# Two decoder layers in one program: layers without a barrier, the root mean square applied at the bank, rotary halves swapped by transfers, weights contiguous in order of use

## The reference, cut to what matters

```python
def hybrid_layer(x, ...):                       # x is (1, 512, 1024), float32; DEPTH = 2 layers
    h = rms_norm(x, ln_g)                       # x * rsqrt(mean(x*x) + eps) * ln_g
    u = einsum('bsd,de->bse', h, w_in)          # 20*256 + 4 + 4*1024 columns
    o_sb = stick_breaking_attention(q_sb, k_sb, v_sb)                       # 4 heads of 64
    o_fx = forgetting_attention(rms_norm(q_fx), rms_norm(k_fx), v_fx, log_f)
    o_dl = dilated_mixture(rope(rms_norm(q_dl)), rope(rms_norm(k_dl)), v_dl)  # 12 heads
    o_mm = memory_cross_attention(rms_norm(q_mm), km, vm)   # km, vm from rms_norm(mem)
    y_b = (o_b * silu(z_b)) @ w_br_b            # for each of the four branches b
    merged = sum_b sigmoid(gate_b) * y_b
    return x + merged @ w_out
```

## Time and profile before

| | |
|---|---|
| median of 3 runs | 1473.55 us (1472.71 to 1476.11) |
| the profiled execution | 1473.23 us, of which the span is 1471.4 us |
| mean granted clock | 0.966 of 2.4 GHz |
| DMA | 115.68 MB, mean 79 GB/s |

### The profile page before, as it was taken

How to read it: one execution, slowest core, us unless ns; L and a number is a source line. 1 busy time by engine, 2 the same in 40 slices (tenths; PEclk the granted TensorE clock), 3 DMA queues, 4 the chain that set the end, 5 groups by cost and what they waited for, 6 DMA issues and landing times.

```text
span 1471.4 us, 18405 instructions
## 1 busy us (share of the span) xinstructions
PE 1366.6 (93%) x6264; PEld 1051.6 (71%) x6264; DVE 506.0 (34%) x762; ACT 688.0 (47%) x1278; POOL 708.7 (48%) x586
## 2 busy tenths in 40 slices
PE   6998999998999999999979899999889999999997
PEld 4766867865667788887757578777656668888876
DVE  5687231233331122222248843213332301222232
ACT  4554522476444544444335534226654445444432
POOL 5556631343332366676355566213432424676662
PEclk8999999998999999999989989999899999999998
DMA  5422321121222144444243224112112222344432
GB/s 177 124 74 65 102 63 37 36 51 43 51 58 56 46 110 104 108 109 115 72 124 101 65 72 108 35 31 51 44 49 52 58 57 64 99 110 108 104 115 96
DMA packets 206974, 115.68 MB, mean 79 GB/s; under 512 B 8212, under 2 KB 200980, under 8 KB 206872
## 3 DMA queue, kind: packets, MB, share of 16 engines
q1 hardware_dynamic: 206872, 114.42, 29.6%
HBM read 108.10 MB, written 6.29 MB: 78 GB/s over the span
## 4 chain that ended last, share of the span: by engine, by line
PE 49%; issue 18%; POOL 14%; DVE 8%; ACT 7%; DMA 2%; SPq 1%; ACTq 0%; POOLq 0%; DVEq 0%
PE dense L715 32%; PE score L715 9%; POOL w_lo L1596 7%; PE acc L715 3%; POOL normed L1629 3%; ACT w_hi L1118 3%; DVE turned L1438 3%; PE out L715 2%; DMA w_raw<-in_w_in 2%; POOL o_norm L1637 1%; POOL inv_den L1637 1%; PE turn L715 1%; DVE negmax L1481 1%; POOL dk_lo L1641 1%; PE turn L840 1%
## 5 line engine op out<-in xcount | busy, mean ns | idle before, releaser
L1596 POOL TENSOR_TENSOR w_lo<-w_raw,w_hi 128x512 fp32r<-128x512 f32 (+1 forms) x398 | 481.9, 1219 | 611.4 <-ACT w_hi L1118 595.7
L715 PE MATMUL dense<-h_hi,w_hi 128*128 128x512 f32 x1168 | 507.7, 435 | 29.9 <-DVE h_lo L1327 15.9
L715 PE MATMUL dense<-h_lo,w_hi 128*128 128x512 f32 x1168 | 466.2, 399 | 0.0
L715 PE MATMUL dense<-h_hi,w_lo 128*128 128x512 f32 x1168 | 466.0, 399 | 0.0
L715 PEld LDWEIGHTS dense<-h_hi,w_hi 128*128 128x128 f32 x1168 | 225.9, 193 | 116.4 <-DVE h_lo L1327 19.0
L715 PEld LDWEIGHTS dense<-h_lo,w_hi 128*128 128x128 f32 x1168 | 226.0, 194 | 50.6 <-issue 11.5
L715 PEld LDWEIGHTS dense<-h_hi,w_lo 128*128 128x128 f32 x1168 | 225.3, 193 | 50.8
L1118 ACT ACTIVATE w_hi<-w_raw 128x512 fp32r<-128x512 f32 (+1 forms) x398 | 225.9, 586 | 53.9 <-PE dense L715 51.0
L1333 DVE TENSOR_SCALAR sig<-sig 128x512 f32<-128x512 f32 x64 | 48.3, 755 | 262.2 <-ACT sig L1173 262.2
L1247 ACT ACTIVATE probs<-score 128x512 f32<-128x512 f32 (+1 forms) x48 | 27.2, 575 | 110.4 <-PE score L715 110.3
L1382 DVE COPY raw<-dense 128x512 f32<-128x512 f32 (+1 forms) x48 | 31.8, 663 | 118.3 <-PE dense L715 118.3
(11 more groups left out here) (280 smaller groups left out, 1939.5 us busy)
## 6 DMA issues: line engine op xcount, KB each, us to landing
w_raw<-in_w_in SPq DMA_DIRECT2D x296, 256.0 KB, 2.9
w_raw<-in_w_out SPq DMA_DIRECT2D x32, 256.0 KB, 2.8
x_scratch<-v_dil SPq DMA_DIRECT2D x16, 256.0 KB, 3.6
w_raw<-in_w_mem_kv SPq DMA_DIRECT2D x16, 256.0 KB, 2.8
v_dil<-x_scratch SPq DMA_DIRECT2D x16, 256.0 KB, 2.7
silu_z<-in_mem SPq DMA_DIRECT2D x4, 512.0 KB, 4.0
w_raw<-in_w_br_dil SPq DMA_DIRECT2D x16, 128.0 KB, 2.3
w_raw<-in_w_br_sb SPq DMA_DIRECT2D x16, 128.0 KB, 2.2
```

The source lines that it names most:

```text
L715: return nc.tensor.matmul(o, lhsT, rhs, start=start, stop=stop, skip_group_check=True)
L1596: pool.tensor_tensor(w_lo[:, n % SPLIT_SLOTS, c], w_raw[:, n % RAW_SLOTS, c], f(w_hi[:, n % SPLIT_SLOTS, c]), ALU.subtract).then_inc(w_lo_ ...
```

## The change

Seven things are changed.

1. **No barrier.** The hardware loop is gone: both layers are written out one after the other, semaphores count on (`Signal.of(key, ago)`), weight items are numbered through both layers, and `end_layer` and the early loads are dropped.
2. **Root mean square at the bank.** `h` becomes x times the gain alone. It is made as soon as x is there: in layer 0 for each half of the tokens while x is still coming in, in layer 1 behind each `o` tile. Each dense tile computed from h is multiplied by 1/rms (`x_rstd_row`) when DVE reads it from its bank. For normed tiles this takes the place of ACT's two reads (ACT now squares `raw`); for gates it is an added instruction (ACT used to read the bank itself). `x_sum` moves into the first tile of the layer. In layer 0 the sum of squares comes from ACT along the token rows.
3. **Rotary halves by transfers.** The four copies become four transfers SBUF to SBUF of 32 x 512 floats, issued on ACT's queue. `post3` of t+1 issues them; sine, cosine and add move to `post4` of t+1, behind the next tile's first half and ahead of `post2` of t+2; rounding and low part move to a new `post5` behind the second half. `turned` has two buffers, `normed` still one.
4. **Weights.** They are laid out in device memory block after block in order of use, so that a partition's 2 KB are contiguous (four runs of 512 B before). Number and bytes of the loads are the same.
5. **Gates.** `cap` and `log_exp` of a gate move from `post1` to `post2`.
6. **Start and constants.** The first weight item is loaded behind the second quarter of x, the large constants behind the first four items; `pick` is one column for each head, broadcast as the stationary operand.
7. **End.** The transposes of x go between the last `o` tiles: 16 behind the fifth, 12 within the last, 4 behind it; stores are by halves.

The core of the diff:

```diff
@@ plan_layer, dense()
             if h == 0:
-                rope = waiting[4]
+                for r in waiting[4]:
+                    add("post4", r)
+                waiting[5] += waiting[4]
                 waiting[4] = []
                 while len(waiting[2]) >= lag and not (...):
                     waiting[3].append(waiting[2].pop(0))
                     add("post2", waiting[3][-1])
-                for r in rope:
-                    add("post4", r)
             if h == len(t.items) - 1:
                 add("post1", t)
                 for r in waiting[3]:
                     add("post3", r)
+                for r in waiting[5]:
+                    add("post5", r)
...
-    for kt in range(KT):
-        add("h", kt)
-    add("h_end")
-    dense([new(kind, DIL, i) for kind in "qk" for i in range(6)], lag=2)
+    dense([new(kind, DIL, i) for kind in "qk" for i in range(6)], [("room",), ("x_sum",)] + [("room",)] * 14, lag=2)
...
-    dense([new("o", None, dt) for dt in range(KT)])
-    for j in range(EARLY):
-        add("early", j)
-    add("x_sum")
+    dense([new("o", None, dt) for dt in range(HALF + 1)])
+    add("out", 0)
+    dense([new("o", None, dt) for dt in range(HALF + 1, KT - 1)])
+    dense([new("o", None, KT - 1)], [("room",), ("out", 1)])
+    add("out", 2)
@@ sync
+                src = w_stream[g, :, c]
+                sp.dma_start(dst, src).then_inc(w_in_sem[g % RAW_SLOTS], 16)
...
-                for n in range(RAW_SLOTS):
-                    load_item(n, (l + 1) % DEPTH, w_next_in)
-                sp.wait_ge(w_next_in, 16 * RAW_SLOTS)
-                sp.wait_ge(layer_done, 4)
-                sp.sem_clear(range(layer_sems[0].num, layer_sems[-1].num + 1))
-                sp.sem_inc(layer_go, 1)
@@ scalar
                     elif kind == "post1" and s[1].kind == "o":
...
+                        act.activation(h_hi[:, kt, :], xT[:, kt, :], ACT.Copy,
+                                       scale=ln_all[:, (l + 1) * KT + kt:(l + 1) * KT + kt + 1]).then_inc(h_hi_ready.sem, 1)
...
                     elif kind == "post1" and s[1].normed:
-                        act.wait_ge(*w_used.of(t.items[-1]))
-                        act.activation(square[...], bank_[:, 0:t.width], ACT.Square)
-                        wait(act, raw_ring.before(t.n))
-                        act.activation(raw[...], bank_[:, 0:t.width], ACT.Copy).then_inc(squared.sem, 1)
+                        act.wait_ge(*raw_ready.of(t.n))
+                        act.activation(square[...], raw[...], ACT.Square).then_inc(squared.sem, 1)
...
+                    elif kind == "post3" and s[1].rope:
+                        act.wait_ge(*normed_ready.of(t.n))
+                        wait(act, (turned_ring, spare_ring)[i].before(t.n))
+                        for q in range(4):
+                            act.dma_start(turned_of[i][32 * q:32 * q + 32, :], normed[32 * (q ^ 1):32 * (q ^ 1) + 32, :])\
+                                .then_inc(halves_in[i], 16)
@@ vector
+                        if t.of_h:
+                            dve.wait_ge(*x_rstd.of("exp"))
...
+                        elif t.kind == "g":
+                            dve.tensor_tensor(sig_place(t), bank_[:, :], x_rstd_row[:, :], ALU.mult).then_inc(g_kept.sem, 1)
+                        elif t.of_h:
+                            dve.tensor_tensor(raw[...], bank_[:, :], x_rstd_row[:, :], ALU.mult).then_inc(raw_ready.sem, 1)
...
-                    elif kind == "post3" and s[1].rope:
-                        for q in range(4):
-                            last = dve.tensor_copy(turned[32 * q:32 * q + 32, :],
-                                                   normed[32 * (q ^ 1):32 * (q ^ 1) + 32, :])
-                        dve.tensor_tensor(turned[:, :], turned[:, :], rope[:, 1, :], ALU.mult).then_inc(sin_done.sem, 1)
...
+                    elif kind == "post4":
+                        dve.wait_ge(*halves_there(t))
+                        dve.tensor_tensor(swapped, swapped, rope[:, 1, :], ALU.mult).then_inc(sin_done.sem, 1)
+                        dve.wait_ge(*sin_done.of(t.n))
+                        dve.wait_ge(*cos_done.of(t.n))
+                        dve.tensor_tensor(swapped, normed[:, :], swapped, ALU.add).then_inc(rope_done.sem, 1)
@@ gpsimd
-                    elif kind == "post3" and s[1].n in cos_done.n and s[1].normed:
-                        pool.wait_ge(*halves_turned.of(t.n))
+                    elif kind == "post4":
+                        pool.wait_ge(*halves_there(t))
                         pool.tensor_tensor(normed[:, :], normed[:, :], rope[:, 0, :], ALU.mult).then_inc(cos_done.sem, 1)
```

More of the change, by code:

```diff
@@ L41 @@
 ROOM = 5
+CONST_LOADS = 4 + 2 * DEPTH
 F32 = mybir.dt.float32
@@ L84, in raw, with of_h @@
         return self.kind not in ("g", "y", "o")
+    @property
+    def of_h(self):
+        return self.kind not in ("mk", "mv", "y", "o")
 def plan_layer():
@@ L215, in plan_layer @@
     dense([new("y", FOX, KT - 1)])
-    dense([new("o", None, dt) for dt in range(KT)])
-    for j in range(EARLY):
-        add("early", j)
-    add("x_sum")
-    assert all(t.kind == "o" for t in waiting[2])
-    steps = [s for s in steps if s[0] != "split" or s[1] < len(stream)]
+    dense([new("o", None, dt) for dt in range(HALF + 1)])
[3 more added lines that the diff above has]
+    add("out", 2)
+    assert all(t.kind == "o" for t in waiting[2]) and not any(waiting[i] for i in (3, 4, 5))
     return steps, tiles, stream
 class Signal:
+    now = 0
     def __init__(self, sem, keys):
@@ L449, in build @@
         ones_set = signal("ones_set", [0])
-        raw_ready = signal("raw_ready", posts(1, lambda t: t.raw and not t.normed))
+        raw_ready = signal("raw_ready", posts(1, lambda t: t.raw))
+        f_raw = signal("f_raw", [0])
+        g_kept = signal("g_kept", posts(1, lambda t: t.kind == "g"))
         sig_exp = signal("sig_exp", posts(1, lambda t: t.kind in ("z", "g")))
@@ new lines, in first_square, with first_high @@
+            def first_square(i):
+                act.wait_ge(x_tok_in[i], 16)
+                if i:
+                    act.wait_ge(first_squares, i)
+                act.activation(flat(square[:, :, :]), token_stage(i), ACT.Square, accum_out=first_ms[:, i:i + 1])\
+                    .then_inc(first_squares, 1)
+            def first_high(u):
+                act.wait_ge(x_placed, 4 * u + 4)
+                c = slice(u * MEM, (u + 1) * MEM)
+                for kt in range(KT):
+                    act.activation(h_hi[:, kt, c], xT[:, kt, c], ACT.Copy, scale=ln_all[:, kt:kt + 1]).then_inc(first_h_hi, 1)
@@ L1103, in log_exp @@
+            act.preload_act_table_set("natural_log_exp_and_others")
+            first_square(0)
+            first_split(0)
+            first_square(1)
+            act.wait_ge(params_in, 16 * DEPTH)
+            first_high(0)
+            first_square(2)
+            first_split(1)
+            first_high(1)
+            first_square(3)
+            first_split(2)
+            act.wait_ge(setup, 2)
+            for l in range(DEPTH):
+                Signal.now = l
                 def log_exp(t):
@@ L1654, in _, with weights_in_order @@
                             .then_inc(plus_lo.sem, 1)
-                end_layer(pool, l)
+def weights_in_order(w_in, w_mem_kv, w_out, w_br):
+    stream = plan_layer()[2]
+    blocks = np.zeros((DEPTH, len(stream), P, HALF * P), np.float32)
+    for n, (name, half, col) in enumerate(stream):
+        w = w_br[name] if name in BRANCHES else {"in": w_in, "kv": w_mem_kv, "out": w_out}[name]
+        rows = 2 * P if name in BRANCHES else HALF * P
+        part = w[:, half * rows:(half + 1) * rows, col:col + P].reshape(DEPTH, rows // P, P, P)
+        blocks[:, n, :, 0:rows] = part.transpose(0, 2, 1, 3).reshape(DEPTH, P, rows)
+    return blocks.reshape(DEPTH * len(stream), P, HALF * P)
 def kernel(x, mem, ln_gain, mem_ln_gain, qk_gain, w_in, b_forget, w_mem_kv,
```

610 lines of the change are left out of this document (286 added, 324 removed).

## The result

The changed kernel takes 1487.78 us (median of 4 runs, 1485.42 to 1488.61) against 1474.83 of the kernel before on the same chip: a ratio of 1.0086, 95% interval 1.0067 to 1.0106. It is slower, by 13 us, where 1467 was forecast with a range up to 1487. The profiled execution took 1488.4 with a span of 1486.6, so 15.2 us more than that of before.

What follows compares the result with a forecast made beforehand. PE, busy for 93%, was at its peak in dense stretches; the ring through `normed` paced the rotary tiles. From 1473.23 us, -7.4 (start) -17.5 (barrier) -7.2 (end) +26.2 (rotary tiles) gave 1467 us, range 1441 to 1487.

Steps and rivals of the forecast that it cites:

- the issue: Rotary tiles, ACT's queue: issuing one transfer takes 0.37 us, 1.48 for four; each 0.1 us is worth 8.4 us.
- B: ACT's queue and the wait for the halves: issues or landings are dear, 1487 at 0.61 an issue; chance 0.25.
- turning point: Rotary tiles: from an issue of 0.44 us or a period of 9.4 the gains at start, barrier and end are used up.
- The links of the rotary ring: Rotary tiles: instructions chained through the one buffer `normed` set the pace, 9.1 us a tile against 7.76 before.
- Rotary tiles of a layer: Twelve rotary tiles per layer: 14.0 us lost, 1.0 more in layer 0, 1.4 back behind them; together 26.2 lost.
- Start: From the start to the first tile's end: first product at about 18.7, tile end at 27.0, 7.4 us saved.
- Barrier: Between the layers: h is made behind each `o` tile and PE waits for nothing, 17.5 us saved.
- End: Behind the last `o` product: 28 of 32 transposes stand ahead of it, 7.2 us saved.
- Gates and attention at nothing: Gate columns and attention stretches: the added bank multiplies and the shift from ACT to DVE cost 0.
- rival D: Gate columns: the added multiply is uncovered, 16 x 0.68 = 11 us more, 1478; chance 0.06.
- Rival A: ACT's queue: issues are cheap, 0.1 us each, giving a period of 8.0 and 1444 us; chance 0.17.
- rival C: Rotary tiles: the ring isn't as described and PE sets the pace of 6.3 us, 1408 us; chance 0.07.

Runs made afterwards that it cites:

- the eight issues: The changed kernel with eight transfers of 32x256 on ACT in place of four of 32x512, same bytes: 1553.69 us, ratio 1.0535 to the kernel before.
- the one: The changed kernel with one 128x512 transfer on ACT in place of four of 32x512, halves not swapped: 1443.42 us, ratio 0.9792 to the kernel before.
- the version with copies: The changed kernel with the swap by four DVE copies and the old order around it again: 1437.57 us, ratio 0.9754 to the kernel before.

## Why the prediction was wrong

The step that failed is one term: "For the issue ... I take 0.37, the commonest of them". It measured 0.61. That is 0.24 us too little, four times for each of 12 tiles in a layer: ten periods, the first cosine, and the last tile, whose way to the cosine (the 4.0 behind the last `normed`) holds four issues too. That makes 0.24 x 4 x 12 = 11.5 us in each layer, 23 in both, and the sum with it 1467.3 + 23 = 1490.3; the profiled execution took 1488.4. The steps below make up the 1.9 between them: some 2 us more in start, barrier, end and rotary tiles, some 4 less behind the rotary tiles of layer 1. The prediction put 0.1 us of an issue at 8.4 us of time. By its own path it is 9.6: 8.0 for twenty periods, 0.8 for the two first cosines and 0.8 for the two last tiles. That B's 1487 came so near the 1487.78 measured is thus in part luck: its price was 3 us too low, and 4 us came back where nobody expected them. This is the case called B, priced at 1487 and given 0.25, and its turning point (an issue of 0.44, a period of 9.4) is passed on the side that it said.

The value was not unknown: the earlier trace rows had 0.61 beside 0.37 and 0.51. I chose the commonest row, a weight load, although the sum hung on it with 8.4 us (rightly 9.6) for each 0.1. The reason given, that it is the commonest, says nothing of the nearness of the two operations, and I ranked none of the three by it. The range ended at 1487, B's own value, without the width that the other terms have, and the measured 1487.78 lies above it.

The other steps, one by one:

- *The links of the rotary ring* hold. The path from the first issue is 2.44, rounding, weight split, `w_lo`, cosine, 5.00 in all where 4.0 + 0.96 was due; the cosine waits for `w_lo` and not for the landing, as said. The landing of 2.1 measured 2.0. The period with 0.61 by the prediction's formula is 9.1 + 0.96 = 10.06; it measured 10.25. Of the other 0.2 the largest piece is the first issue, 0.08 behind the square's start; the rest are 0.04 in a few handovers.
- *Rotary tiles of a layer*: 15.0 - 1.4 = 13.6 forecast for layer 0, 25.1 with the right issue; measured 25.7, two long groups of issues included. For layer 1, without the 1.0 for the constants, 12.6 forecast and 24.1 with the right issue; measured 24.3.
- *Start*: -7.4 forecast, -6.9 measured. First product at 18.30 (18.7), first bank read at 27.72 (27.0). In part luck: PE took 6.9 us to the end of the tile (25.17), not 7.9, since its products went at 0.43 for nine of them and not twelve; and the read came 2.5 us behind that, because DVE waited for ACT's 1/rms, which the prediction didn't have in this path.
- *Barrier*: -17.5 forecast, -16.8 measured. PE goes from the last `o` into layer 1 with no gap; the bank is read at 757.35 because 1/rms comes then, which PE doesn't feel.
- *End*: 5.8 from last product to the span's end forecast, 6.4 measured; transposes 3.3 forecast, 3.1 measured. Net -7.2 forecast, -7.1 measured.
- *Gates and attention at nothing*: from the rotary tiles to the last x of layer 0 the difference is -0.1. The window from 600 to 700, answering to the earlier trace rows, now holds 439 matmuls, 0.228 each. The 426 of before aren't its like: that window reaches past the columns, over a wait of PE until 692.40; from 590 to 690 before has 435, 0.230 each, and that, not 0.235, was the columns' pace:

```profile
600.00:700.00 100.00, 100.00 (x439) 81.83 (x438) 27.52 (x47) 50.17 (x93) 70.34 (x64) 1.00 0.39 110
```

  So the columns with the added multiplies are no slower (PE stood 1.0 of 180 us before, from 509.73, and not at all after), and rival D is excluded. What they gained in layer 0 was lost again in the attention stretches by this sum; it fits that over the span the waits of PE for `o_norm` went from 11.8 to 14.2 us and for `negmax` from 7.8 to 8.5.
- *Layer 1, behind its rotary tiles*: at nothing in the forecast, -4.1 measured, where the same stretch of layer 0 has -0.1. The change is the same in both layers, so it is probably not the change. Cut into twelve equal windows, this stretch has a mean granted clock of 0.972 before and 0.978 after in layer 1, and 0.978 and 0.975 in layer 0. The clock may be the cause, and no run shows it.

Rival A (cheap issues) needed 0.1 us each, and they took 0.61; rival C (the ring isn't the bound) is excluded by the eight issues and the one: the period followed the queue's time in full.

What the prediction did not see, since I had read only the four copies as one line and their mean of 0.67, is that the copies of 2.70 were 1.7 of copying and 1.0 of waiting for POOL. I took the 2.70 as the price of what was removed. With the bank multiply in front, a swap on DVE takes 2.17 (and 1.7 with no `w_lo` beside it), so that transfers had even less to win. It doesn't enter the sum of the changed kernel, only that of the version with copies, which I put 9 us too high.

## What to carry to other kernels

A transfer between SBUF buffers cost the queue that issued it some 0.5 to 0.6 us here, for 32 KB as for 256, and everything queued behind it moved by that. Count issues, not bytes, and put them on a queue behind which nobody waits. Where a short ring over one buffer sets the pace, moving a link to an engine that is fuller by its busy share may still gain: PE at 94% took over the swap and the kernel got 15 us faster than with copies on DVE.
When a term is worth several us for each 0.1 us of a row, the row has to be chosen by its likeness (who issues, how many rows, from where to where), and where none is like it, the range has to reach past the dearest of them.

## What the runs showed of the hardware that I had not expected

An issue of a transfer from SBUF to SBUF of 32 rows takes 0.60 to 0.63 us in most cases (2.41 to 2.52 for four) and up to 0.80 in a few (3.21 for four), with 2 KB or 1 KB a row, on ACT or SP; one of 128 rows takes 0.47. The form with fewer rows is the dearer. Why isn't settled; no run varied the rows alone. The Trainium skill, page "DMA: Bandwidth & Descriptors", section "Issuing engines are not separate DMA queues", calls the sequencer's time for an issue usually small relative to the DMA; here one issue (0.61) is near a third of the 2.0 from issue to landing, and four in a row (2.44) take longer than it, so the measurement decides.

A copy of 32x512 on DVE takes 0.42 us by itself and up to 1.42 when a `w_lo` was ahead of it, and a group's mean (0.67) hides it. In the kernel with the copies one takes 2.16: it starts at 117.40 under a `w_lo` (116.71 to 117.98), a MEMSET of POOL follows directly (117.91, 1.38), and it ends 0.27 behind that. The same happened to the scaling of the memory's tokens, which took 1.77 to 1.84 for each of its two halves in the changed kernel where it now stands beside POOL's work, 0.7 before:

```profile
145.14 3.53 DVE L1364 TENSOR_SCALAR silu_z<-silu_z,negmax 128x1024 f32<-128x1024 f32 x2
```
